# Expert sums by stacked diagonals of 32 columns: four slots of 32 tokens in each gathered block

## The reference, cut to what matters

```python
idx = jnp.take_along_axis(cand_i, pos, axis=-1)      # (token, head, 16)
gate = jax.nn.softmax(best_s, axis=-1)
u = expert_u[it]                                     # (token, 128, 1024)
h = jax.nn.gelu(jnp.einsum('td,tkd->tk', xt, u), approximate=False)
v = expert_v[it]
y = jnp.einsum('tk,tkd->td', gt * h, v)
```

## Time and profile before

| | us |
|---|---|
| median of three runs | 1856.92 (1856.31 to 1864.26) |
| span of the profiled execution (its own time is not given apart from that) | 1861.1 |
| TensorE matmul busy | 1615.5 (87%) |
| VectorE busy | 993.2 (53%) |
| ScalarE busy | 461.4 (25%) |
| GpSimd busy | 320.3 (17%) |
| mean rate of the DMA engines | 253 GB/s |

### The profile page before, as it was taken

How to read it: one execution, slowest core, us unless ns; L and a number is a source line. 1 busy time by engine, 2 the same in 40 slices (tenths; PEclk the granted TensorE clock), 3 DMA queues, 4 the chain that set the end, 5 groups by cost and what they waited for, 6 DMA issues and landing times.

```text
span 1861.1 us, 19442 instructions
## 1 busy us (share of the span) xinstructions
PE 1615.5 (87%) x7700; PEld 1078.6 (58%) x7700; DVE 993.2 (53%) x1843; ACT 461.4 (25%) x1018; POOL 320.3 (17%) x269
## 2 busy tenths in 40 slices
PE   7999989999897986889867666667999999899998
PEld 6857756764845544346423222226998476489963
DVE  2433334331776777258996666563566415346654
ACT  1152152230233544123333322221000013310001
POOL 0000000000112544233554545520000000000000
PEclk9999999999998998999988998898999999999999
DMA  6444221126898799999999999993544533154443
GB/s 234 174 147 176 91 91 46 53 95 224 316 407 340 311 422 398 410 423 412 413 420 421 420 422 422 421 398 141 208 158 150 209 150 131 59 204 181 165 153 113
DMA packets 55192, 471.32 MB, mean 253 GB/s; under 512 B 6592, under 2 KB 7744, under 8 KB 10432
## 3 DMA queue, kind: packets, MB, share of 16 engines
q0 software_dynamic: 36864, 268.45, 35.0%
q1 hardware_dynamic: 18240, 201.66, 28.7%
HBM read 469.04 MB, written 1.05 MB: 253 GB/s over the span
## 4 chain that ended last, share of the span: by engine, by line
PE 64%; DMA 17%; DVE 11%; ACT 4%; issue 3%; POOL 1%; SPq 0%; DVEq 0%; ACTq 0%; POOLq 0%
PE ps L2385 13%; DMA main<-in_expert_uv,main 11%; PE ps L489 7%; PE ps L445 6%; PE ps L1014 6%; PE ps L2542 5%; PE ps L415 5%; DMA panels<-in_expert_uv,main 4%; PE ps L1252 4%; PE ps L2312 3%; DVE main L942 3%; PE ps L485 2%; PE ps L2308 2%; PE ps L2331 2%; PE ps L1486 2%
## 5 line engine op out<-in xcount | busy, mean ns | idle before, releaser
L1014 PE MATMUL ps<-main 128*128 128x512 f32 x672 | 331.8, 643 | 95.9 <-ACT main L989 95.7
L924 POOL DMA_INDIRECT main<-in_expert_uv,main x206 | 250.7, 1217 | 378.1 <-PE ps L1014 215.1
L942 DVE SCALAR_TENSOR_TENSOR main<-main 128x1024 f32<-128x1024 f32 x206 | 246.9, 1222 | 98.5 <-DMA main<-in_expert_uv,main 97.3
L1014 PEld LDWEIGHTS ps<-main 128*128 128x128 f32 x672 | 131.7, 205 | 275.5 <-issue 142.1
L1014 PE MATMUL ps<-panels,main 128*128 128x512 f32 x156 | 82.4, 674 | 50.6 <-ACT main L989 39.8
L977 ACT ACTIVATE main<-main 128x2 f32<-128x2 f32 x128 | 25.9, 202 | 372.8 <-DVE main L942 293.9
L445 PE MATMUL ps<-panels,xT 128*128 128x512 f32 x256 | 112.5, 592 | 0.0
L2385 PE MATMUL ps<-main 128*128 128x128 f32 x912 | 104.9, 275 | 0.0
L2385 PEld LDWEIGHTS ps<-main 128*128 128x128 f32 x912 | 103.4, 192 | 0.0
L489 PE MATMUL ps<-panels,main 128*128 128x512 f32 x192 | 87.9, 618 | 7.3 <-ACT main L547 7.3
L1252 PEld LDWEIGHTS ps<-main 128*128 128x128 f32 x704 | 82.0, 192 | 11.9 <-issue 8.8
(11 more groups left out here) (320 smaller groups left out, 2384.8 us busy)
## 6 DMA issues: line engine op xcount, KB each, us to landing
panels<-in_wall SPq DMA_DIRECT2D x87, 2048.0 KB, 8.2
main<-in_rows SPq DMA_DIRECT2D x14, 512.0 KB, 10.1
main<-in_expert_uv,main POOLq DMA_INDIRECT x206, 17.1
main<-in_sub_keys SPq DMA_DIRECT2D x2, 1024.0 KB, 13.3
main<-in_wall SPq DMA_DIRECT2D x1, 2048.0 KB, 12.7
mats<-in_mats SPq DMA_DIRECT2D x1, 1088.0 KB, 5.5
x<-in_x SPq DMA_DIRECT2D x2, 512.0 KB, 4.0
main<-in_pool_w SPq DMA_DIRECT2D x1, 1024.0 KB, 31.6
```

The costliest lines, as they stand in the source:

```text
L924: pool.indirect_dma_start(out=self.bufs[self.buf_of[r]], out_offset=None, in_=self.c.dram["expert_uv"], in_offset=bass.IndirectOffsetOnAxi ...
L942: dve.scalar_tensor_tensor(out=u, in0=u, scalar=1.0, in1=self.c.row(m, H2), op0=ALU.mult, op1=ALU.mult, accum_out=self.dots_at[:, m, q:q + ...
L1014: mm = pe.matmul(self.c.ps[:, b, :], self.diags[self.of_pe(r) % DIAG_RING], v[:, half * HALF:(half + 1) * HALF], start=(q == 1), stop=(q = ...
```

## The change

A block still gathers 128 rows, but they belong to four slots of 32 tokens instead of one slot of 128. Partition 32k + i of block `4s + q` holds slot `4s + k` of token `32q + i`. So

- the diagonal becomes a 128x32 stack of four 32x32 diagonals (`repeat` scaled per partition), and a matmul with it adds four slots of 32 tokens at once into the 32 partitions of the output that start at `32q`. Two blocks are summed together, in the order half, block;
- the dots need each token group's `h2` in all four partition groups: `repeat` makes four copies of 128x1024 per tile on TensorE and ScalarE (`REPEATED`, three more areas of 1024);
- the chosen numbers and gates, made with one token per partition, are brought into the new places: `by_quarter` on VectorE, eight short matmuls on TensorE and two copies on VectorE per group (`spread_out`, stages `spread0` to `spread4`);
- VectorE adds no blocks: `ADDED`, `add` and the add in `finish_vector` go;
- the loads for the pooling of tile 0 go to other areas and wait until tile 0's dots are done; the store for GpSimd's descriptors is set to 4096 bytes per partition.

The same changes that are made in the stages of tile 0 are made in those of tile 1.

```diff
-ADDED = [r for r in range(0, 2 * SLOTS, ADD_EVERY) if not any(a <= r < b for a, b in CHOICES)]
@@ Experts
-        self.diags = [c.row(0, DIAGS)[:, P * n:P * (n + 1)] for n in range(DIAG_RING)]
+        self.diags = [c.row(0, DIAGS)[:, LANES * n:LANES * (n + 1)] for n in range(DIAG_RING)]
@@ dot
+        if q < QUARTERS:
+            dve.wait_ge(*self.c.un.read_out(f"choose{m}.repeat{q}"))
-        dve.scalar_tensor_tensor(out=u, in0=u, scalar=1.0, in1=self.c.row(m, H2), op0=ALU.mult, op1=ALU.mult,
+        dve.scalar_tensor_tensor(out=u, in0=u, scalar=1.0, in1=self.repeated[m][q % QUARTERS], op0=ALU.mult,
@@ weigh
-            act.activation(self.diags[self.of_pe(r) % DIAG_RING], self.c.mat("ident"), ACT.Copy,
+            act.activation(self.diags[r % DIAG_RING], self.c.mat("repeat")[:, 0:LANES], ACT.Copy,
@@ sums_at
+        if r % GROUP != GROUP - 1:
+            return None
         if r < PAIRED:
+            return r + 1 - GROUP
+        return r - BEHIND if r >= PAIRED + BEHIND else None
@@ sum
+        pe.wait_ge(self.diag_made, first + GROUP)
         for half, b in enumerate(banks):
+            for k in range(GROUP):
+                v = self.bufs[self.buf_of[first + k]][:, D:UV]
+                at = LANES * ((q + k) % QUARTERS)
+                mm = pe.matmul(self.c.ps[at:at + LANES, b, :], self.diags[(first + k) % DIAG_RING],
+                               v[:, half * HALF:(half + 1) * HALF], start=(q + k < QUARTERS),
+                               stop=(q + k >= SLOTS - QUARTERS))
@@ tile_tensor, behind scores1
+        for half in range(2):
+            mm = pe.matmul(un.view(x, 2)[:, half, :], c.mat("repeat")[lanes, :],
+                           t.h2[lanes, HALF * half:HALF * (half + 1)], start=True, stop=True)
@@ tile_tensor, spread_out(g)
+        pe.wait_ge(*c.at("named_by_quarter", m, g + 1))
+        for bank, src in enumerate(t.by_quarter):
+            for k in range(QUARTERS):
+                mm = pe.matmul(un.view(x, 2)[LANES * k:LANES * (k + 1), bank, 0:n], c.mat("repeat")[:, 0:LANES],
+                               src[:, n * k:n * (k + 1)], start=True, stop=True)
@@ tile_scalar, behind scores1
+        act.activation(t.repeated[q], un.view(x, 2).rearrange("p b n -> p (b n)"), ACT.Copy).then_inc(un.freed(x), 1)
@@ tile_vector
+        if g > 1:
+            spread_out(g - 1)
+            yield f"spread{g - 1}"
+        if g in (0, len(GROUPS) - 1):
+            spread_out(g)
+            yield f"spread{g}"
@@ mixers_order
+    part("tile0", "pq0a", "scores0", "pq0b", "scores1", "repeat", "top0", "best0", "name0", "spread0")
+    part("tile0", "pq2", "pq3", "scores3", "spread1")
+    part("tile0", "spread2")
+    part("tile0", "spread3", "top4", "best4", "name4", "spread4")
@@ second_early_sync
+    sp.wait_ge(c.experts.dotted, SLOTS)
@@ kernel
+    nc = bacc.Bacc("TRN2", target_bir_lowering=False, num_devices=1, dynamic_dma_scratch_size=4096)
```

More of the change, by code:

```diff
@@ L95 @@
 BESIDE[0] += [(x, q, j) for x in BOTH for q in range(2) for j in range(2)]
-MATS = (["ident", "upto", "after", "ones"]
+MATS = (["ident", "upto", "after", "ones", "repeat"]
         + [f"span{l}" for l in range(LEVELS)] + [f"level{l}" for l in range(LEVELS)])
@@ L109, in constant_matrices @@
     p, i = np.meshgrid(np.arange(P), np.arange(P), indexing="ij")
-    out = [p == i, p <= i, p > i, np.ones((P, P))]
+    out = [p == i, p <= i, p > i, np.ones((P, P)), p % LANES == i % LANES]
     spans, levels = [], []
@@ L891, in place @@
         self.last_in_panels = [last[n] for n in self.panel_bufs]
[L893 to L897, removed]
     def wait_used(self, eng, r):
[L901 to L904, removed]
+        eng.wait_ge(self.summed, r + 1)
     def gpsimd(self, pool):
@@ L1023, in finish_vector @@
         end = (m + 1) * SLOTS
-        dve.wait_ge(rows.added, rows.of_dve(end))
-        x = c.x[:, m, :].rearrange("p (a b) -> p a b", b=P)
-        dve.tensor_tensor(x, x, rows.y(m), ALU.add).then_inc(c.dve_chain.next(), 1)
-        dve.wait_ge(rows.summed, rows.of_pe(end))
-        dve.wait_ge(*c.dve_chain.made())
+        dve.wait_ge(rows.summed, end)
         for half in range(2):
@@ L1050, in hgrn_units @@
     return units
-CHOOSE_UNITS = {f"scores{g}": [f"scores{g}"] for g in range(len(GROUPS))}
+CHOOSE_UNITS = {f"{x}{g}": [f"{x}{g}"] for x in ("scores", "spread") for g in range(len(GROUPS))}
+CHOOSE_UNITS["repeat"] = [f"repeat{q}" for q in range(QUARTERS)]
 class Delta:
@@ L1645, in tile_tensor @@
     yield "scores1"
+    for q in range(QUARTERS):
+        repeat(q)
+    yield "repeat"
     for g in range(len(GROUPS)):
@@ L1709, in tile_scalar @@
     yield "scores1"
+    for q in range(QUARTERS):
+        x = t.un(f"repeat{q}")
+        act.wait_ge(*un.full(x))
+        act.activation(t.repeated[q], un.view(x, 2).rearrange("p b n -> p (b n)"), ACT.Copy).then_inc(un.freed(x), 1)
+    yield "repeat"
     for g, (first, n) in enumerate(GROUPS):
@@ L1764, in tile_vector @@
     yield "norm"
-    for stop in ("pq0a", "scores0", "pq0b", "scores1"):
+    for stop in ("pq0a", "scores0", "pq0b", "scores1", "repeat"):
         yield stop
@@ L1822, in tile_vector @@
                                       op0=ALU.mult, op1=ALU.add))
-        dve.tensor_copy(t.experts[:, TOPK * first:TOPK * (first + n)].bitcast(U32),
-                        named[0].rearrange("p h k -> p (h k)")).then_inc(c.up("experts_named"), 1)
+        by_quarter(t.by_quarter[0], named[0], n).then_inc(chain.next(), 1)
         dve.wait_ge(*c.at("gate_exp", m, g + 1))
@@ L1967, in mixers_order @@
     part("tile0", "best1", "name1")
-    part("tile0", "pq2", "pq3", "scores3")
+    part("tile0", "pq2", "pq3", "scores3", "spread1")
     rows(2)
@@ L1993, in mixers_order @@
     part("read1", 5)
-    part("tile0", "top4", "best4", "name4")
+    part("tile0", "spread3", "top4", "best4", "name4", "spread4")
     rows(4)
@@ L2025, in mixers_order @@
     rows(2)
-    part("tile1", "name0", "pq1", "scores2")
+    part("tile1", "name0", "spread0", "pq1", "scores2")
     rows(2)
@@ L2042, in mixers_order @@
         part("tile1", f"name{g}")
+        if g == 4:
+            part("tile1", "spread4")
         rows(3)
```

121 lines of the change are left out of this document (67 added, 54 removed).

## The result

The changed kernel takes 1905.79 us, the median of four runs (1901.60 to 1907.37), beside 1858.34 us for the kernel before: a ratio of 1.0247, 95% interval 1.0228 to 1.0265. It is slower by 47 us, on the side that was forecast, 16 us above the predicted 1890, inside the range, and 0.8 us above the 1872 to 1905 that the prediction gave to its own account alone. The profiled execution took 1901.6 us with a span of 1899.6, the shortest of the four. Its span is 38.5 us longer than the 1861.1 of before.

What follows compares the result with a forecast made beforehand. Gather bytes bound 650 to 1240 us, engine order the time before; 27 - 3 + 12 - 2.5 = +33.5 us gave a span of 1894.6, or 1890 us from the median of the runs; range 1857 to 1920.

Steps and rivals of the forecast that it cites:

- (a) to (f): Steps through tile 0's choice, from the repeats to the sums ahead of hgrn1: delay growing to +27 us.
- (a): Start of tile 0's choice: repeats and spread0 delay pq1 to 492.8 (+11.1 us) and the first gather to 493.4.
- "After it", to 650: Behind tile 0's choice, up to 650 us: shorter sums fill the queue sooner, -3 us (0 to -5).
- Tile 1's choice: In the full DMA stretch: +22 us at name4 less 10.5 in reserve, +12 (0 to +20).
- in reserve: Tile 1's choice: a block is dotted 16.3 us after issue, a transfer needs an estimated 6; some 10.5 us absorb delay.
- The tail: Last pair of sums, 6.73 us before, takes 4.3 side by side: -2.5 us (0 without overlap).
- The pair of sums: TensorE's matmuls for two blocks overlap in different quarters: 2.1 us a pair, 3.4 if not.
- Costed at nothing: VectorE's dropped additions, the smaller descriptor store and SyncE's later loads: 0 us, at most 5 for the loads.
- Rival 1: TensorE's sums don't overlap: +58 us, 1915 us; chance 0.22.
- Rival 2: Faster: waits at the spreads cost little and halved sums decide, about -15 us, 1842 us; chance 0.12.
- Rival 3: Nothing visible: shift of 10 to 15 us at block 12's dots, less 8 from shorter sums, 1860 us; chance 0.13.
- rival 4: Descriptor store too short, gathers queue, a block every 2.7 instead of 2.49 us: +54, 1911 us; chance 0.03.

Runs made afterwards that it cites:

- experiment 1: Kernel before, with TensorE and VectorE only waiting for each other at the five spread places of each tile, no data moved: 1882.5 us, ratio 1.0132.
- experiment 2: Changed kernel with VectorE's copies of spread1 to spread3 moved behind the next group's top, in both tiles: 1877.55 us, ratio 1.0104.
- experiment 12: Changed kernel with only tile 1's spreads, copies and repeats moved later, tile 0 untouched: 1888.49 us, ratio 1.0161.
- experiment 4: Changed kernel with the two loops of a sum exchanged, block outside and half inside: 1898.85 us, ratio 1.0231.
- experiment 10: Kernel before with no additions on VectorE, all 256 blocks summed on TensorE with 128-column diagonals: 1858.51 us, ratio 1.0011.
- experiment 11: Kernel before with the descriptor store set to 4096 bytes per partition, nothing else: 1856.28 us, ratio 0.9999.
- experiment 9: Changed kernel, both tiles reordered: copies, repeats and tile 1's spreads later; tile 0's name2 ahead of hgrn1's f, blocks 12 to 15 behind top4: 1853.43 us, ratio 0.9983.
- the kernel before in the new order: Kernel before with name2 ahead of hgrn1's f and blocks 12 to 15 behind top4, nothing of the change: 1849.46 us, ratio 0.9954.
- experiment 8: Changed kernel with all blocks' sums written to the first quarter of the output's partitions, results wrong: 1931.91 us, one run.

## Why the prediction was right, and where it was off

**Tile 0's choice, (a) to (f): right.** Less the 3.2 us by which this execution came to it late, `pq1` started at 491.5 (forecast 492.8), the first gather at 492.1 (493.4), `spread1` was over at 521.8 (522.8), VectorE's wait for the `b_f` panels at 546.2 (546), its wait at `spread2` at 564.5 (564.5), `top4` started at 597.4 (594.8), the dots of block 12 at 615.2 (612.9), and `hgrn1` at 624.8 (621 to 623). Experiments 1 and 2 show the cause and not only the times. The 2.6 us that came on by `top4` are the clock: the pair at 587.79 took 3.62 and the panel at 591.34 took 8.37 where I had 2.1 and 7.3. In experiment 12, with tile 0 in the same order and the same 3.29 us of idle time ahead, the same pair took 1.91 and the panel 7.41. In (a) a size was off: the repeats take 2.5 us for 8 records, not 3.5. The shift came out right all the same, because TensorE and ScalarE take turns at them: TensorE waits 0.57 us for a copy, ScalarE 1.53 and 1.16 us for TensorE, and the last copy ended at 488.6 where I had 489.6.

**"After it", to 650: right in size, but not where I looked for it.** I gave back 3 us and had GpSimd's long wait end near 635; it ended at 646.6. From `hgrn1`'s start to that issue the changed kernel took 18.6 us, the kernel before 17.3. The pair that releases it, after and before:

```profile
642.32 3.63 PE L994 MATMUL ps<-main 128*32 128x512 f32 x8 [3.53 <-ACT main L963]
```

```profile
608.19 6.59 PE L1014 MATMUL ps<-main 128*128 128x512 f32 x8 [3.38 <-ACT main L989]
```

The new pair is shorter by 3 us, but GpSimd waits for its first block. Before, that block was summed in the middle of the pair, and the issue came 4.1 us after the pair's start; now both are done at its end, and it came 4.3 us after. The shorter sums helped further on: the transfers of block 96 are 26.5 us late where `hgrn1` was 29.9, 3.4 us less, and the forecast for them was 24. With tile 0 in the same order it was 22.6 in experiment 12 and 22.8 in 4.

**Tile 1's choice: the sum right, two of its terms off.** Forecast +12, measured +13.1 between the dots of blocks 96 and 255, and 10.1 of it gone in experiment 12. But the +12 was +22 at `name4` less 10.5 in reserve. The dot of block 128, the first work behind `name4`, was late by 17.7 more than that of block 96, and 4.6 of that did not reach the transfers. The reserve had been taken too large: the block that GpSimd issued at 958.47 was issued at 1008.08 in the changed kernel and dotted as it landed at 1018.38, 10.3 us later, where the prediction needed an estimated 6 for a transfer. So at most 6.0 of the 16.3 us were in reserve. That the two errors nearly cancel is luck. Besides, that row names VectorE's first addition of tile 1 (`L952`) as what released GpSimd, not `name4`; the change has no additions. The DMA share did not stay at 1.0.

**The tail: right in kind, and in part by luck.** Forecast -2.5, measured -3.4 between the dot of block 255 and the end of the last sum. The last pair took 3.15 us for the 6.73 of the earlier trace rows. Experiment 1 has the old sums, and its last pair is shorter all the same, by 3.0 (after, then experiment 1):

```profile
1302.83 3.15 PE L994 MATMUL ps<-panels,main 128*32 128x512 f32 x8 [3.00 <-ACT main L963]
```

```profile
1281.86 3.70 PE L1014 MATMUL ps<-panels,main 128*128 128x512 f32 x8 [2.80 <-ACT main L989]
```

So most of the 6.73 us was the clock of that one execution, and at the full clock the overlap is worth 1.8 us here (1.91 for 3.70).

**The pair of sums: right in size, wrong in one reason.** 1.91 us against 2.1. But I took the overlap from the order of the loops, and experiment 4 shows that the order gives nothing. What the Trainium skill says in "TensorE: Matmul & The Clock Gate", Part 3, of matmuls in different column groups, the trace bears out: 1.91 for 3.62 us, 1.9 times. The drain that the Trainium skill, "TensorEngine Tiling", Key Properties, puts at a change of the tiling mode shows in no row: the pair at 548.64 stands without idle time between full-width panels and takes 1.91 us.

**Costed at nothing:** the additions, the descriptor store, SyncE's later loads. Experiments 10 and 11 confirm the first two; the third was not tried alone, and is in experiment 9, which is 0.3% slower than the kernel before in the new order.

**The median.** The terms give +33.5 us of span, measured +38.5: of the 5 us, 3.2 lie ahead of the change's place, for which there was no term. The other 10 of the 16 us come from the way to the median: the profiled span of before lay 4.2 above its median, that of after 6.2 below. That is the scatter of single executions, and no term of the sum could know it.

**Rivals.** Rival 1 (no overlap, 25 us more than mine) did not happen; experiment 8 prices it at 26, by one execution. Rival 2 asked for under 5 us at the dots of block 12; it was 33. Rival 3 asked for 10 to 15 there, and rival 4 is excluded by experiment 11.

**Open.** The changed kernel in its best order (experiment 9) has its last sum 2.3 us ahead of the kernel before in the new order (1253.20 and 1255.47), and yet is 0.3% slower by the two ratios, with 596.7 us behind that sum for 593.1. No run tells whether that is scatter. Nor is it known why tile 1's choice was longer with its repeats split. How the loss divides between the waits and the added work isn't shown either: experiment 1 gives the waits alone 24 us, experiment 2 gets 28 back by order alone, and the two overlap.

## What to carry to other kernels

A small exchange between two engines costs by its place in their orders, not by its size: ask for each wait what stands ahead of it on the other engine, and let the receiver take up its result only where the work after it needs it. Walking both queues with measured durations, step by step, gave the start of `hgrn1`, some 120 us on, to within 4 us. Judge such a sum term by term, and at the engine that sets the time: here the transfers tell which delays count, and two terms of tile 1's part were 4 to 6 us too large and nearly cancelled. When a reordering helps the changed kernel, try the same order on the kernel before, or its gain is put down to the change.

## What the runs showed of the hardware

- Two float32 matmuls with diagonals of 32 columns overlap when they write different quarters of the output's partitions, in both orders that were tried (1.91 and 1.92 us a pair of blocks, 3.62 in one quarter). Products of 32 rows overlap too: 8 records of the repeats take 1.99 us in one place and 2.52 in another, where 8 full ones take 3.5 by the earlier trace rows (0.44 each).
- The time that shorter sums freed went partly into the clock: in 1060 to 1240 TensorE was busy for 104.07 us at a granted clock of 0.75 after the change, for 114.37 at 0.91 before, and for 141.97 at 0.99 in experiment 8, where the same sums don't overlap; all three between the levels of 1.2 and 2.4 GHz. The last pair after the change, behind 3.00 us of idle time, took 3.15 us; at the full clock it would be 1.91.
